# Attention scores in three passes over rounded parts, whole first transfers, and a reordered first strip

## The reference, cut to what matters

```python
# block 1
h = rmsnorm(x, pre_mix_w); proj = h @ w_in           # 1024 -> 5120
y_a = diff_attention(q_a, k_a, v_a, lam, ...)         # 4 heads, each two softmaxes over 64 dims
y_b = neighbourhood_attention_2d(q_b, k_b, v_b, rpb)  # 8 heads of 64 dims
merged = g_a * (y_a @ w_branch_a) + g_b * (y_b @ w_branch_b)
x = x + rmsnorm(merged @ w_out, post_mix_w)
x = x + rmsnorm((silu(h @ w_gate) * (h @ w_up)) @ w_down, post_ffn_w)
# block 2: latent attention (8 heads of 96 dims, causal) beside a gated linear attention, then the same kind of FFN
q = concat([q_nope, rope(q_rope)]) * 96 ** -0.5
s = where(mask, q @ k.T, -inf); o = softmax(s) @ v
```

## Time and profile before

| What | us |
|---|---|
| Median of three runs (753.23 to 753.76) | 753.26 |
| The profiled execution | 753.9 |
| Its span in the trace | 752.2 |
| PE busy | 745.2 (99% of the span) |
| DVE busy | 480.9 (64%) |
| ACT busy | 402.2 (53%) |

### The profile page before, as it was taken

How to read it: one execution, slowest core, us unless ns; L and a number is a source line. 1 busy time by engine, 2 the same in 40 slices (tenths; PEclk the granted TensorE clock), 3 DMA queues, 4 the chain that set the end, 5 groups by cost and what they waited for, 6 DMA issues and landing times.

```text
span 752.2 us, 10167 instructions
## 1 busy us (share of the span) xinstructions
PE 745.2 (99%) x3847; PEld 618.6 (82%) x3847; DVE 480.9 (64%) x742; ACT 402.2 (53%) x607; POOL 54.4 (7%) x127
## 2 busy tenths in 40 slices
PE   9999999999999999999999999999999999999997
PEld 7887877888888888888898888888888888888886
DVE  5576766666956665774376877576865575566633
ACT  5646766544744444554368555676345455455422
POOL 1100100000460000000023000200002000000000
PEclk9999999999999999999999999999999999999999
DMA  8855454555656656546476373444464565555541
GB/s 317 269 184 212 137 173 136 191 171 179 220 172 196 192 167 201 196 157 206 127 237 200 110 240 118 126 154 129 147 216 154 190 202 165 193 192 174 195 140 57
DMA packets 57231, 134.34 MB, mean 179 GB/s; under 512 B 7831, under 2 KB 13278, under 8 KB 57182
## 3 DMA queue, kind: packets, MB, share of 16 engines
q1 hardware_dynamic: 56528, 132.16, 54.1%
q10 hardware_dynamic: 654, 1.53, 0.6%
HBM read 132.61 MB, written 1.05 MB: 178 GB/s over the span
## 4 chain that ended last, share of the span: by engine, by line
PE 98%; DMA 1%; DVE 0%; SPq 0%; ACT 0%; POOL 0%; issue 0%; ACTq 0%; POOLq 0%
PE acc L1113 87%; PE aux L1038 4%; PE aux L1216 1%; PE aux L1178 1%; PE aux L1251 1%; DMA x<-in_x_dram 1%; PE aux L1197 1%; PE acc L1104 1%; PE aux L1326 1%; PE aux L1241 0%; PE aux L1104 0%; PE aux L1356 0%; PE aux L1366 0%; PE aux L1341 0%; PE aux L1303 0%; PE aux L1306 0%
## 5 line engine op out<-in xcount | busy, mean ns | idle before, releaser
L1113 PE MATMUL acc<-weights_high,h_high 128*128 128x512 f32 (+1 forms) x720 | 229.3, 394 | 0.0
L1417 DVE SCALAR_TENSOR_TENSOR weights_low<-weights_raw,gain_columns,weights_high 128x1024 fp32r<-128x1024 f32 (+3 forms) x189 | 218.5, 1189 | 15.2 <-ACT weights_high L682 15.1
L1113 PE MATMUL acc<-weights_high,h_low 128*128 128x512 f32 (+1 forms) x720 | 224.3, 387 | 0.0
L1113 PE MATMUL acc<-weights_low,h_high 128*128 128x512 f32 (+1 forms) x720 | 223.9, 387 | 0.0
L682 ACT ACTIVATE weights_high<-weights_raw,gain_columns 128x1024 fp32r<-128x1024 f32 (+3 forms) x188 | 194.6, 1074 | 19.8 <-DMA weights_raw<-in_w_in_dram 11.7
L1113 PEld LDWEIGHTS acc<-weights_low,h_high 128*128 128x128 f32 x720 | 134.4, 188 | 27.6
L1113 PEld LDWEIGHTS acc<-weights_high,h_low 128*128 128x128 f32 x720 | 134.3, 188 | 27.5 <-DVE h_low L1436 0.4
L1113 PEld LDWEIGHTS acc<-weights_high,h_high 128*128 128x128 f32 x720 | 130.7, 188 | 25.4 <-issue 1.9
L1414 DVE TENSOR_TENSOR weights_low<-weights_raw,weights_high 128x1024 fp32r<-128x1024 f32 x68 | 81.0, 1220 | 35.9 <-ACT weights_high L682 35.7
L682 ACT ACTIVATE weights_high<-weights_raw 128x1024 fp32r<-128x1024 f32 x68 | 69.7, 1057 | 48.1 <-DMA weights_raw<-in_ffn_w_down_dram 22.6
L738 ACT ACTIVATE silu_tmp<-acc,stats 128x512 f32<-128x512 f32 (+1 forms) x24 | 15.7, 654 | 88.4 <-PE acc L1113 88.4
(11 more groups left out here) (269 smaller groups left out, 637.4 us busy)
## 6 DMA issues: line engine op xcount, KB each, us to landing
weights_raw<-in_w_in_dram SPq DMA_DIRECT2D x59, 512.0 KB, 5.1
weights_raw<-in_w_gate_dram SPq DMA_DIRECT2D x44, 256.0 KB, 3.4
weights_raw<-in_w_up_dram SPq DMA_DIRECT2D x44, 256.0 KB, 4.0
weights_raw<-in_w_down_dram SPq DMA_DIRECT2D x22, 512.0 KB, 4.6
weights_raw<-in_ffn_w_gate_dram SPq DMA_DIRECT2D x44, 256.0 KB, 3.3
weights_raw<-in_ffn_w_up_dram SPq DMA_DIRECT2D x44, 256.0 KB, 4.1
weights_raw<-in_ffn_w_down_dram SPq DMA_DIRECT2D x22, 512.0 KB, 4.8
weights_raw<-in_w_out_dram SPq DMA_DIRECT2D x16, 512.0 KB, 4.6
```

The source lines that it names most:

```text
L1113: i = nc.tensor.matmul(acc[:, 2 * t + b, 0:width], lhs[:, k0, sl], w[:, u % RING, base + d:base + d + width], start=(kt == 0 and n == 0), ...
L1417: i = nc.vector.scalar_tensor_tensor(lo[:, u % RING, c], raw[:, u % RING, c], gcol[:, g:g + 1], hi[:, u % RING, c].bitcast(F32), ALU.mult, ...
```

## The change

Scores: q and k of all three attentions are kept as a high and a low part in float32r, and each score product becomes three accumulated passes (high q with high k, low q with high k, high q with low k). In a pair the passes alternate over the two heads; in the latent attention a head's three passes follow each other. DVE makes the low parts: for q of the differential attention four operations of 128 columns a tile, for everything else one of 512 columns a bank. PE's reuse of the transposes' banks then waits for the low part. The latent scores of tile 0 wait for tile 0's transposes alone, no longer for tile 1's. The latent probabilities use the buffer of the output gate (`silu_og`), after it has been read.

Start: x comes in two transfers of 512 KB (one a tile), the first unit in one of 512 KB on ACT's queue; `warm` is 4. The first strip is written out (`first_products`): tile 0's high-high and low-high, tile 1's transposes, tile 1's high-high, tile 0's high-low, tile 1's low-high and high-low. DVE makes strips 0 and 1 of tile 0 high and low at once, strips 2 and 3 in a later step `rest_of_first`.

```diff
-    out.append(do("warm", 8))
-    run("qk_a", [1, 1, 2, 4], {(0, 0): [do("norm_turn", "mix", 1, 0)], (0, 2): [do("norm_turn", "mix", 0, 1)],
+    out.append(do("warm", 4))
+    run("qk_a", [1, 1, 2, 4], {(0, 0): [do("norm_turn", "mix", 1, 0), do("rest_of_first")], (0, 2): [do("norm_turn", "mix", 0, 1)],
...
-            qaT = sb1("q_a_T", [P, DA_HEADS, SEQ])
+            qaT = [sb1(f"q_a_{part}", [P, DA_HEADS, SEQ], F32R) for part in ("high", "low")]
...
-            T2 = sb("probs_2", [P, 2, 512], F32, s)
...
+            T2 = sil
...
-            load_x(0, 0)
-            sp.dma_start(raw[:, 0, 512:1024], dram["w_in"][0, 0:P, 512:1024]).then_inc(*tick("raw_loaded0", 0, 16))
-            load_x(1, 0)
+            load_x(0)
+            load_x(1)
             weights(1)
             weights(2)
             weights(3)
-            load_x(0, 1)
-            load_x(1, 1)
...
-            act.dma_start(raw[:, 0, 0:512], ins["w_in"][0, 0:P, 0:512]).then_inc(*tick("first_loaded", None, 16))
+            act.dma_start(raw[:, 0, :], ins["w_in"][0, 0:P, 0:1024]).then_inc(*tick("first_loaded", None, 16))
...
+            def first_products():
+
+                def passes(t, lhs, w):
+                    for b in range(2):
+                        c = slice(512 * b, 512 * b + 512)
+                        if t == 0 and lhs is hT[0]:
+                            pe.wait_ge(*at("high_ready" if w is hi else "low_ready", (0, 0) if b else "left"))
+                        i = nc.tensor.matmul(acc[:, 2 * t + b, :], lhs[:, 0, t * P:(t + 1) * P], w[:, 0, c],
+                                             start=(lhs is hT[0] and w is hi), stop=False)
+                    return i
+
+                pe.wait_ge(*at("turned_high_vec", "mix_first"))
+                passes(0, hT[0], hi)
+                pe.wait_ge(*at("turned_low", "mix_first"))
+                passes(0, hT[1], hi)
+                step("norm_turn", "mix", 1, 0)
+                pe.wait_ge(*at("turned_high", ("mix", 1, 0)))
+                passes(1, hT[0], hi)
+                passes(0, hT[0], lo)
+                pe.wait_ge(*at("turned_low", ("mix", 1, 0)))
+                passes(1, hT[1], hi)
+                passes(1, hT[0], lo).then_inc(*tick("weights_used", 0))
...
-                        for hb in range(2):
-                            m = nc.tensor.matmul(scores(kind, i, hb), att_q(kind, hb, i), att_k(kind, hb, i),
-                                                 start=True, stop=True)
+                        for n, (pq, pk) in enumerate(((0, 0), (1, 0), (0, 1))):
+                            for hb in range(2):
+                                m = nc.tensor.matmul(scores(kind, i, hb), att_q(kind, hb, i, pq), att_k(kind, hb, i, pk),
+                                                     start=(n == 0), stop=(n == 2))
...
-                    if i == 0:
-                        pe.wait_ge(*at("turned_out", ("mla", 1, 3)))
+                    if i % 4 == 0:
+                        pe.wait_ge(*at("turned_low", ("mla", i // 4, 3)))
...
                     for hb in range(2):
-                        m = nc.tensor.matmul(scores(kind, i, hb), att_q(kind, hb, i),
-                                             att_k(kind, hb, i), start=True, stop=True)
+                        for n, (pq, pk) in enumerate(((0, 0), (1, 0), (0, 1))):
+                            m = nc.tensor.matmul(scores(kind, i, hb), att_q(kind, hb, i, pq), att_k(kind, hb, i, pk),
+                                                 start=(n == 0), stop=(n == 2))
...
+            def first_strips(k, bank, key):
+
+                high, low = (part[:, k:k + 2, 0:P] for part in hT)
+                src = aux[bank][:, 0:2 * P].rearrange("p (k s) -> p k s", k=2)
+                dve.wait_ge(*at("turned", key))
+                signal(nc.vector.tensor_copy(high, src), "turned_high_vec", key, True)
+                nc.vector.tensor_tensor(low, src, high.bitcast(F32), ALU.subtract).then_inc(*tick("turned_low", key))
...
+                    for n in range(4):
+                        i = nc.vector.scalar_tensor_tensor(
+                            qaT[1][:, n, s], aux[2 * t][:, n * P:(n + 1) * P], -HD ** -0.5 * 4.0 ** (n + 1),
+                            qaT[0][:, n, s].bitcast(F32), ALU.mult, ALU.subtract)
+                    i.then_inc(*tick("vec", ("q_a", t)))
+                    dve.wait_ge(*at("turned_out", ("k_a", t)))
+                    nc.vector.tensor_tensor(kaT[1][:, :, s], aux[2 * t + 1][:, :].rearrange("p (k s) -> p k s", k=4),
+                                            kaT[0][:, :, s].bitcast(F32), ALU.subtract)\
+                        .then_inc(*tick("vec", ("k_a_low", t)))
...
+                elif kind == "mla_turn":
+                    t, = a
+                    for b in range(4):
+                        dve.wait_ge(*at("turned_high", ("mla", t, b)))
...
+                        nc.vector.tensor_tensor(low, aux[b][0:MLA_QK, :].rearrange("p (k s) -> p k s", k=4),
+                                                high.bitcast(F32), ALU.subtract)\
+                            .then_inc(*tick("turned_low", ("mla", t, b)))
```

More of the change, by code:

```diff
@@ L369, in program @@
         with ExitStack() as att1:
-            qaT = sb1("q_a_T", [P, DA_HEADS, SEQ])
-            kaT = sb1("k_a_T", [P, DA_HEADS, SEQ])
+            qaT = [sb1(f"q_a_{part}", [P, DA_HEADS, SEQ], F32R) for part in ("high", "low")]
+            kaT = [sb1(f"k_a_{part}", [P, DA_HEADS, SEQ], F32R) for part in ("high", "low")]
             va = sb1("v_a", [P, TOKS, 512])
-            qbT = sb1("q_b_T", [P, 4, SEQ])
-            kbT = sb1("k_b_T", [P, 4, SEQ])
+            qbT = [sb1(f"q_b_{part}", [P, 4, SEQ], F32R) for part in ("high", "low")]
+            kbT = [sb1(f"k_b_{part}", [P, 4, SEQ], F32R) for part in ("high", "low")]
             vb = sb1("v_b", [P, TOKS, 512])
@@ L401, in program @@
             gb2 = sb("gates_b2", [P, TOKS, D], F32, s)
-            qmT = sb("q_latent_T", [MLA_QK, MLA_H, SEQ], F32, s)
-            kmT = sb("k_latent_T", [MLA_QK, MLA_H, SEQ], F32, s)
-            T2 = sb("probs_2", [P, 2, 512], F32, s)
+            qmT = [sb(f"q_latent_{part}", [MLA_QK, MLA_H, SEQ], F32R, s) for part in ("high", "low")]
+            kmT = [sb(f"k_latent_{part}", [MLA_QK, MLA_H, SEQ], F32R, s) for part in ("high", "low")]
             PT2 = sb("probs_T_2", [P, 2, 512], F32, s)
@@ L501, in slot_free, with att_q @@
             return ("mm_done", (name, TOKS - 1)) if kt + PER.get(name, 1) == SC[name][2] else ("weights_used", u)
-        def att_q(kind, hb, i):
+        def att_q(kind, hb, i, part=0):
             qt, n = divmod(i, 4)
@@ L507, in att_q, with att_k @@
             if kind == "mla":
[L508 to L511 removed]
+                return qmT[part][:, 2 * n + hb, s_]
+            return (qaT if kind == "da" else qbT)[part][hb * HD:hb * HD + HD, n, s_]
+        def att_k(kind, hb, i, part=0):
             qt, n = divmod(i, 4)
             if kind == "mla":
[L514 to L515 removed]
+                return kmT[part][:, 2 * n + hb, 0:(qt + 1) * P]
+            return (kaT if kind == "da" else kbT)[part][hb * HD:hb * HD + HD, n, :]
         def att_keys(kind, i):
@@ L1089, in product @@
                 for n, (lhs, w) in enumerate(passes):
-                    if u == 0 and t == 0 and lhs is xl:
-                        step("norm_turn", "mix", 1, 0)
                     if t == 0 and w is lo:
@@ L1164, in step @@
                     turn((kind[:3], t), bank_of[kind[:3], t], slices(row[:, t, 0:512], 4),
-                         ("turned_out", (kind[:3], t)))
+                         ("vec", (kind[:3] + "_low", t)))
                 elif kind == "pair":
@@ L1602, in step @@
                         if (tag, t, b) == ("mix", 0, 0):
[L1603 to L1614 removed]
+                            first_strips(0, 1, "mix_first")
                             continue
@@ L1617, in step @@
                                    0.5 if tag.startswith("merged") else 1.0)
+                elif kind == "rest_of_first":
+                    first_strips(2, 0, ("mix", 0, 0))
                 elif kind == "gain_turn":
@@ L1849, in step @@
                            "sumsq_vec", ("gla", t))
+                elif kind == "mla_turn":
+                    t, = a
+                    for b in range(4):
+                        dve.wait_ge(*at("turned_high", ("mla", t, b)))
+                        high, low = (part[:, 4 * (b % 2):4 * (b % 2) + 4, t * P:(t + 1) * P]
+                                     for part in (qmT, kmT)[b // 2])
+                        nc.vector.tensor_tensor(low, aux[b][0:MLA_QK, :].rearrange("p (k s) -> p k s", k=4),
+                                                high.bitcast(F32), ALU.subtract)\
+                            .then_inc(*tick("turned_low", ("mla", t, b)))
                 elif kind == "gla_heads":
```

65 lines of the change are left out of this document (32 added, 33 removed).

## The result

The changed kernel takes 755.78 us, the median of 5 runs (755.24 to 758.03), against 753.26 for the kernel before (5 runs beside it): ratio 1.0037, 95% interval 1.0025 to 1.0049. So it is slower, by 2.5 us on the medians. The forecast was 753.4 and "no change"; 755.78 lies in its range (751.6 to 756.4), near the upper end, and two of the five runs (757.43 and 758.03) lie above it. The profiled run has 755.24 and a span of 753.5, 1.3 longer than before.

A forecast was written before the change was run, and what follows sets the result against it. It took PE to bound the kernel. Start +0.7, pairs -1.1, wide latent scores -0.6 and narrow ones +1.1 summed to +0.1 us on the median of 753.26, hence 753.4, with a range of 751.6 to 756.4.

The forecast's parts named there:

- the narrow passes: Rival in the 128-column latent scores: a float32r pass costs 0.216 us, +3.4 in place of +1.1, giving 755.7; 15%.
- a late DVE: Rival: DVE late at the latent transposes or the second unit, +1.9 us, giving 755.3; 7%.
- 15 + 10 + 3, most of the 7 and 2% of the forecast: Percent chances of slower: narrow passes, pairs not side by side, clock, late DVE, and the forecast's own upper end.
- The start: From the first transfers to the second unit: later x and new order cost +0.7 us, bounds 0 to 1.6.
- The order: First strip, from tile 1's transposes to the second unit: 3.26 us in place of 3.11, +0.15.
- The clock rival: At the start: a thinner start drops PE to 1.2 GHz, the first strip's 12 products double, +2.7, 756.1; 3%.
- The pairs: Scores on 64 partitions: 12 float32r passes side by side take 0.92 us, 0.14 less; -1.1 us over 8 pairs.
- the rival of 759.1: In the pairs: 64-row float32r passes do not run side by side, +4.6 us in place of -1.1; 10%.
- The wide latent scores: Latent scores i = 4 to 7: 16 records of 0.216 us become 24 passes of 0.12, -0.6 us.
- The narrow latent scores: Latent scores i = 0 to 3, 128 moving columns: 24 passes of 0.12 us, 2.9 against 1.78, +1.1 us.
- DVE (0): New low parts on DVE, densest before the latent scores: covered by its 4.82 us of idle time, cost 0.

The follow-up runs named there:

- experiment 4: The changed kernel with 15 zero products instead of 7 at the start: 755.29 us, ratio 1.0019 to the kernel before.
- experiments 5 and 7: 5: kernel before with whole transfers or new order, separately or both transfers (754.33 to 756.18 us); 7: changed kernel, gains ahead of unit 0 (758.42; 15 zero products 755.73).
- experiment 6: The kernel before with x and unit 0 in whole transfers, the old order and 15 zero products instead of 7: 755.14 us.
- experiment 3: The kernel before with 2 zero products instead of 7 and nothing else: 755.37 us, ratio 1.0019.
- experiment 1: The changed kernel with the start of before (half transfers, eight fills, old order), so three-pass scores alone: 752.63 us, ratio 0.9987.

## Why the prediction was right and wrong

The range held the result, but the likeliest case, 753.4 with no change, did not come. That the range held it is in part luck: it reached so far up for the narrow passes and a late DVE, neither of which came, and two of the five runs lie above it. Its chances were added up wrongly too: 15 + 10 + 3, most of the 7 and 2% of the forecast come to about 0.35 for slower by more, where it says 0.29, so it thought the case that came less likely than its own rivals make it. By its terms:

- **The start (+0.7, bounds 0 to 1.6) failed, by 1.5 us.** Its step was the landing of x at 5.7 and from there 1.36 to the first product: x landed at 5.8, almost as reckoned, but nothing in the sum asked about the gains, whose transpose is ahead of x's on PE. They are 4 KB, and before they were through in the shade of the zeros. Their path has to be followed like that of x: 1.75 us of standing, to 6.20, with it the fills and first products at half rate, and ACT's high part of unit 0 put off to 6.82. The first two products, put at 0.23 each, take 0.86 in the new order even at full rate (experiment 4), because the second waits for ACT's right half. At the second unit that is +2.2, outside the bounds given; the kernel with the scores of before measured +4.8.
- **The order (+0.15) came as reckoned**, read as it was reckoned, from tile 1's transposes to the second unit: 3.11 before, 3.24 in the changed kernel (9.56 to 12.80), 3.23 with the new order alone (7.53 to 10.76). The idle time of 0.69 behind tile 1's transposes is in every timeline of the new order, and DVE's low parts were in time.
- **The clock rival (3%) is part of the mechanism that came true, and it was dismissed on a row that does not show it.** I took "PEclk 1.00" in the first window for proof that PE ran at 2.4 GHz. It prints 1.00 in the changed kernel too, where products took twice their time until 9.0 (stretch; busy us and instructions of PE, PEld, DVE, ACT, POOL; PEclk; DMA share; GB/s):

```profile
7.50:10.00 2.50, 2.50 (x12) 2.12 (x11) 1.77 (x4) 0.66 (x2) 0.00 (x0) 1.00 1.03 420
```

  The spacing of the records shows what PE did: in both kernels the records of the zero products start 0.21 apart (from 1.47 on), where with 15 of them the same records come 0.11 apart from 4.65 on (experiment 4). Both kernels begin at half rate, the level of 1.2 GHz. In the kernel before it is over at 5.7 (eight fills in 0.89); in the changed one PE stands from 4.45 to 6.20, and the half rate goes on to 9.0. A fall from full rate is printed, as 0.50, in experiments 5 and 7; the half rate of the first records is not. The Trainium skill, page "TensorE: Matmul & The Clock Gate", section "What's actually happening", says that the default is the throttled state and activity releases it. By record spacing the trace agrees (0.21 against 0.11), and my sentence that it does not was wrong. The rival's price, 12 products doubled or +2.7, was about twice what the rate cost in most runs: 1.0 in experiment 6, 1.2 to 1.6 in experiment 3 (1.5 at the second unit and 1.9 on the medians, less 0.3 for x), more where the stretch ran on to 15.3. That its 756.1 is near the result is chance, since the later gains make up the rest.
- **The pairs (-1.1)**: -1.4, 0.17 a pair, passes side by side every 0.117. The forecast's 0.92 a pair was 0.89; the rival of 759.1 is out.
- **The wide latent scores (-0.6)**: 24 passes of 0.12. From start to next product the first group shows 1.52 against 1.54; but the neighbours come closer too. From the transposes ahead of it to the third product group behind it, the changed kernel has 2.86 (504.60 to 507.46), before it was 3.13 (502.72 to 505.85), and the second group 3.24 against 3.53: -0.56.
- **The narrow latent scores (+1.1)**: 0.111 a pass for my 0.12; read in the same wide way +0.42 and +0.49, +0.9. The rival at 0.216 a pass (15%) is out. These 24 passes take 2.67 us. By the 81 ns of the Trainium skill (same page, section "Back-to-back issue gap") they would take an estimated 1.94 us; the measurement differs and decides, 0.111 for these float32r passes. Plain float32 needs two records per product of the same 0.111, three passes cost half as much again: the three-pass form loses at 128 columns and wins at 256.
- **DVE (0)** held. Its low parts fill the gap, and no wait of PE names DVE there:

```profile
481.10 1.28 DVE L1895 TENSOR_TENSOR q_latent_low<-aux,q_latent_high 96x512 fp32r<-96x512 f32 x2 [0.66 <-ACT q_latent_high L965]
...
489.18 1.27 DVE L1437 SCALAR_TENSOR_TENSOR weights_low<-weights_raw,gain_columns,weights_high 128x1024 fp32r<-128x1024 f32 x1
490.38 0.28 DVE L1693 CUSTOM_DVE_ANT_0 silu_og_probs<-aux,causal 128x128 f32<-128x128 f32 x1
```

The 4.82 us of idle time before the scores are gone, as foretold; the price is nil.

The scores by these terms: -1.4 - 0.56 + 0.9 = -1.06; experiment 1 measured -1.05 (span -1.1). That half of the prediction stands. With +2.2 for the start the sum is +1.1, against +1.3 in the spans of the two profiled runs. The medians say +2.5: the profiled run of the changed kernel is 0.5 below its median, the lowest of five, and that of the kernel before 0.6 above its own.

## What to carry to other kernels

At the start, follow every transfer that the first instructions of the bounding engine need, the smallest too: 4 KB behind larger transfers came 1.3 to 2.1 us later, and cutting 512 KB transfers in halves was worth 2.5 to 2.7 us of 753. Before lengthening a transfer, ask what stands behind it on all queues, which other engines need it (here ACT's first weights wait for the gains), and whether PE has work until it lands; a PE that stood some 2 us lost another 1 to 1.6 us at half rate, and more where that ran on. Passes over high and low parts pay where the moving side is wide; judge each shape by its own record spacing, and take the version with the scores alone here (752.6).

## What the runs showed of the hardware that was not expected

- The printed granted clock does not show the half rate at which a kernel begins: it is 1.00 while the records of the zero products start 0.21 apart, and still 1.00 when the same records come 0.11 apart from 4.65 us on (experiment 4). It does show a later fall from full rate: 0.50 from 8 to 10 us with x whole, and from 10 to 16 with the gains in front. Record spacing shows both.
- Every profiled kernel begins at half rate. In the kernel before, without a pause, it was over by 5.7 us, ahead of the first product. Where PE stood for 1.4 to 2.2 us, full rate came for good at 9.0, 9.8, 10.3, 11.0, 11.3, 15.3 or 16.6 us in seven kernels with much the same start. In three of them (x whole, both whole, the gains in front) PE came back from the pause at full rate and fell 1.2 to 1.5 us after it. What decides how long it lasts was not settled.
- The same 4 KB transfer, issued at 1.23 in each, was in use at 4.5 with 512 KB issued ahead on two queues in halves of rows, at 5.85 and 6.23 with 768 KB, one transfer in whole rows, and at 6.2 to 6.6 with 1024 KB in whole rows.
- A float32r pass costs 0.111 at 128 columns and 0.12 at 256: below 256 columns the moving side hardly counts.
